# Expert rows weighted at eviction and added to the residual by an adding DMA, in a float32 hybrid-decoder layer

## What is computed

```python
x = x + mix                                    # residual after attention ("x2" in the kernel)
h = rms_norm(x, norm_ffn)                      # "h2"
g_probs = softmax(h @ w_group + b_group)       # 4 groups; top group g_idx with g_p = max
e_sel   = e_logits[tok, g_idx]                 # 8 experts of that group
top_v, top_i = lax.top_k(e_sel, 2)
top_w   = softmax(top_v) * g_p[:, None]        # the two weights of a token
# rows sorted by expert, every expert padded to blocks of 128 rows
yr = (silu(xb @ w_gate[e]) * (xb @ w_up[e])) @ w_down[e]
y  = zeros.at[row_tok].add(yr * row_w[:, None])
out = rms_norm(x + y, norm_final)
```

## Time and profile before

| | us |
|---|---|
| median of three runs | 2680.06 (2677.91 to 2688.39) |
| the profiled execution, its time | 2681.16 |
| its span from first to last instruction | 2679.6 |
| PE busy | 2340.3 (87%) |
| DVE busy | 1420.9 (53%) |
| ACT busy | 1188.9 (44%) |
| POOL busy | 663.5 (25%) |
| moved by DMA | 473.65 MB, 177 GB/s over the span |

### The profile page before, as it was taken

One profiled execution on the slowest core, in us unless ns is written; L12 is line 12 of the kernel. 1 busy time (PEld: TensorE's weight loads), 2 busy tenths in 40 slices (PEclk: granted clock), 3 DMA queues, 4 the chain that ended last, 5 costly groups with the idle time before them and its releaser, 6 DMA issues. The chain is left out here.

```text
span 2679.6 us, 36979 instructions
## 1 busy us (share of the span) xinstructions
PE 2340.3 (87%) x11480; PEld 1874.8 (70%) x11480; DVE 1420.9 (53%) x2814; ACT 1188.9 (44%) x1605; POOL 663.5 (25%) x464
## 2 busy tenths in 40 slices
PE   5999999994999999999959998399999999999920
PEld 3888889993666666666637887277888888787810
DVE  6212211004666666766634665476655565757656
ACT  5011111113666666667632222275555555556623
POOL 0000000003676666666600111110111111111133
PEclk7999999996999999999979998599999999999965
DMA  5333334215345453553145442579876776878668
GB/s 181 134 110 130 113 125 113 61 45 141 89 119 131 120 138 97 132 128 99 48 132 188 123 123 84 219 277 354 300 276 243 266 278 237 300 304 301 256 231 325
DMA packets 228011, 473.65 MB, mean 177 GB/s; under 512 B 20073, under 2 KB 72465, under 8 KB 225874
## 3 DMA queue, kind: packets, MB, share of 16 engines
q1 hardware_dynamic: 203026, 391.00, 43.7%
q0 software_dynamic: 17072, 53.79, 6.1%
q10 hardware_dynamic: 7824, 27.79, 2.8%
HBM read 355.30 MB, written 117.21 MB: 176 GB/s over the span
## 5 line engine op out<-in xcount | busy, mean ns | idle before, releaser
L1338 DVE TENSOR_TENSOR gu_lo<-gu_raw,gu_hi 128x2048 fp32r<-128x2048 f32 x128 | 293.2, 2291 | 130.9 <-issue 57.8
L584 DVE TENSOR_SCALAR_CACHE_REDUCE p_ring<-ps_s 128x256 f32<-128x256 f32 (+7 forms) x352 | 277.8, 793 | 156.3 <-PE ps_s L655 151.3
L521 POOL TENSOR_TENSOR p_ring<-p_ring 128x1152 f32<-128x1152 f32 (+15 forms) x128 | 322.1, 2516 | 10.7
L549 ACT ACTIVATE p_ring<-p_ring,shift 128x1152 f32<-128x1152 f32 (+15 forms) x256 | 305.9, 1197 | 27.2 <-DVE shift L600 27.2
L690 PE MATMUL ps_o<-aT,v_st 128*128 128x512 f32 (+3 forms) x640 | 291.1, 539 | 0.0
L1268 ACT ACTIVATE gu_hi<-gu_raw 128x2048 fp32r (+1 forms) x128 | 237.5, 1908 | 81.7 <-PE ps_g L1431 43.8
L538 ACT ACTIVATE aT<-ps_t 128x512 f32<-128x512 f32 (+1 forms) x320 | 168.3, 532 | 226.0 <-PE ps_t L675 225.9
L655 PE MATMUL ps_s<-k,q_st 128*128 128x512 f32 (+3 forms) x640 | 209.1, 454 | 45.8 <-DMA near<-near_rows 24.4
L1431 PE MATMUL ps_g<-gu_hi,xT_lo 128*128 128x512 f32 x720 | 231.8, 403 | 5.9 <-DVE xT_lo L1353 5.4
L1431 PE MATMUL ps_g<-gu_hi,xT_hi 128*128 128x512 f32 x720 | 227.8, 397 | 0.0
L1431 PE MATMUL ps_g<-gu_lo,xT_hi 128*128 128x512 f32 x720 | 227.7, 397 | 0.0
(11 more groups left out here) (224 smaller groups left out, 4211.2 us busy)
## 6 DMA issues: line engine op xcount, KB each, us to landing
gu_raw<-in_moe_w_gate SPq DMA_DIRECT2D x128, 512.0 KB, 11.7
gu_raw<-in_moe_w_up SPq DMA_DIRECT2D x128, 512.0 KB, 12.6
d_raw<-in_moe_w_down SPq DMA_DIRECT2D x64, 1024.0 KB, 5.0
qk<-stage SPq DMA_DIRECT2D x64, 512.0 KB, 2.8
q_st<-qk SPq DMA_DIRECT2D x128, 256.0 KB, 5.1
y_rows<-y_sb ACTq DMA_DIRECT2D x45, 512.0 KB, 6.9
y_rows<-nil SPq DMA_DIRECT2D x32, 512.0 KB, 6.1
w_raw<-in_diff_w_in POOLq DMA_DIRECT2D x12, 1024.0 KB, 6.8
```

Of the source, the lines that this page charges most:

```text
L521: pool.tensor_tensor(p0(r, 0, w), p0(r, 0, w), p1(r, 0, w), ALU.add).then_inc(mixed, 1)
L549: nc.scalar.activation(p, p, ACT.Exp, bias=shift[:, r % 8, m:m + 1], accum_out=sums[:, r % 8, m:m + 1]).then_inc(raised, 1)
L584: ins = nc.vector.tensor_scalar(p(r, k0, k0 + far), ps_s[:, c % 2, 0:far], SCALE, None, ALU.mult, ALU.max, accum_out=top[:, r % 4, m, col: ...
L1338: nc.vector.tensor_tensor(gu_lo[:, j * GC:(j + 1) * GC], raw(half, j), gu_hi[:, j * GC:(j + 1) * GC].bitcast(F32), ALU.subtract).then_inc( ...
```

## The change

Three groups of edits, made together.

**Weights early, in the lists.** An entry of `slots` is now a pair (token, weight). `choose` forms two differences on DVE (`x5`); ACT takes their exponential (`e5`) in the middle of its step, for tile n-5; `place` forms the sum, the reciprocal and the product and puts them beside the token (`tokw`). `kept`, `e_all`, `rank_all`, `start` and `dest` are no longer carried on, and three small copies in `choose` and one in `place` go. Empty entries are not zero but a dump row, 2048 plus a lane number, with weight 0; for that `h2` and `x2` get 128 more rows, which `attend` clears with two writes, and the 32 writes to `y` go, with `y` itself. The table has an eighth column.

**Adding in the expert stage.** `take_y` evicts with the row's weight as scale, and instead of the store POOL issues an indirect DMA that adds `y_sb` to the rows of `x2` that the list names. Because the list of block b+3 is loaded when block b+1 is added, lists wait in a line of five (`lists`), passed on by two POOL copies for each block (`pass_on`). `take_y` waits for these copies (`held`), and the copies wait for the add before (`y_out`). The transposes of the next block's rows move into the middle of `gate_up`.

**A shorter last stage.** `finish` loads all 16 tiles of `x2` at once, norms and stores them; no ring, no gathers, no weights.

```diff
@@ attend, SP
-            spare = scratch["y"].rearrange("(b p) d -> b p d", p=P)[EXPERTS:]
+            for dump in (scratch["h2"], scratch["x2"]):
+                sp.dma_start(dump[SEQ:SEQ + P].rearrange("p (k d) -> p k d", k=4),
+                             nil[:, :].unsqueeze(1).to_broadcast([P, 4, D // 4])).then_inc(nil_out, 16)
...
-                if n >= 0 and n % 9 == 5 and cleared < BLOCKS_MAX - EXPERTS:
-                    sp.dma_start(spare[cleared].rearrange("p (k d) -> p k d", k=4),
-                                 nil[:, :].unsqueeze(1).to_broadcast([P, 4, D // 4])).then_inc(nil_out, 16)
-                    cleared += 1
@@ mix_and_route, POOL
-            pool.memset(zeros[:, :], 0).then_inc(made, 1)
+            pool.memset(empty[:, :, :], 0).then_inc(made, 1)
...
+            pool.iota(lanes[:, :], pattern=[[1, SLOTS // P]], base=0, channel_multiplier=SLOTS // P).then_inc(made, 1)
...
+            pool.wait_ge(empty_set, 1)
@@ mix_and_route, ACT step
+                if has(at, 5):
+                    q = 1 - par
+                    act.wait_ge(chosen, (n - 5) * 13 + 13)
+                    nc.scalar.activation(e5[:, q, :], x5[:, q, :], ACT.Exp).then_inc(exped, 1)
+                if has(at, 0):
                     act.wait_ge(turned, n + (1 + TURNED0))
@@ mix_and_route, DVE choose and place
+                nc.vector.tensor_scalar(x5[:, q, 0:GROUPS_E], lg[:, 0:GROUPS_E], gm[:, 0:1], None, ALU.subtract)
...
+                nc.vector.tensor_tensor(x5[:, q, 4:5], ev[:, 1:2], ev[:, 0:1], ALU.subtract)
...
-                nc.vector.tensor_copy(kept[:, bass.ds(t, 1), 0:4].rearrange("p o n -> p (o n)"), lg[:, 0:4])
-                nc.vector.tensor_copy(kept[:, bass.ds(t, 1), 4:6].rearrange("p o n -> p (o n)"), ev[:, 0:2])
-                link(nc.vector.tensor_copy(e_all[:, bass.ds(t, 1), :].rearrange("p o n -> p (o n)"), eid[:, q, :]))
...
-                nc.vector.tensor_copy(rank_all[:, bass.ds(t, 1), :].rearrange("p o n -> p (o n)"), rank[:, q, :])
...
+                gate(dve, exped, t + 1, passed)
+                link(nc.vector.tensor_reduce(e_sum[:, :], e5[:, q, 0:GROUPS_E], AX.X, ALU.add))
+                link(nc.vector.scalar_tensor_tensor(out=den[:, :], in0=e5[:, q, 4:5], scalar=1.0, in1=e_sum[:, :],
+                                                    op0=ALU.add, op1=ALU.mult))
                 dve.wait_ge(freed, t + (FREED0 - 1))
-                link(nc.vector.tensor_copy(tok[:, q:q + 1], tok_f[:, 0:1]))
+                weight = tokw[:, q, :, 1].bitcast(F32)
+                link(nc.vector.reciprocal(weight[:, 0:1], den[:, :]))
+                link(nc.vector.tensor_tensor(weight[:, 1:2], weight[:, 0:1], e5[:, q, 4:5], ALU.mult))
+                nc.vector.tensor_copy(tokw[:, q, :, 0], tok_f[:, 0:1].to_broadcast([P, 2]))
@@ run_experts, POOL
+            def pass_on(count):
+                pool.tensor_copy(lists[:, 0:4, 0], lists[:, 1:5, 0]).then_inc(held, 1)
+                pool.tensor_copy(lists[:, 0:4, 1].bitcast(F32), lists[:, 1:5, 1].bitcast(F32)).then_inc(held, 1)
+                gate(pool, held, count * 2 + 1, passed)
+
+            def add_y(k):
+                gate(pool, y_taken, k + Y_TAKEN0, passed)
+                pool.indirect_dma_start(scratch["x2"], bass.IndirectOffsetOnAxis(ap=to_rows[:, 0:1], axis=0),
+                                        y_sb[:, :], None, compute_op=ALU.add).then_inc(y_out, 16)
...
+            for b in range(3):
+                load_x(b)
+                pass_on(b + 1)
+            load_x(3)
+            pass_on(4)
+            add_y(1)
+            with pool.Fori(1, most) as b:
+                load_x(b + 3)
+
+                gate(pool, y_out, b * 16, passed)
+                pass_on(b + 4)
+                add_y(b + 1)
@@ run_experts, ACT take_y (store_y goes)
-                act.wait_ge(y_out, k * 16 + (Y_OUT0 - 16))
-                nc.scalar.activation(y_sb[:, :], ps_y[:, :], ACT.Copy).then_inc(y_taken, 1)
+                act.wait_ge(held, k * 2 + 7)
+                nc.scalar.activation(y_sb[:, :], ps_y[:, :], ACT.Copy, scale=lists[:, 0, 1:2].bitcast(F32)).then_inc(y_taken, 1)
@@ run_experts, PE
                 for c in range(KC):
+                    if c == KC // 2 and ahead is not None:
+                        turn_x(ahead)
...
-                gate_up(b)
-                turn_x(b + 1)
+                gate_up(b, b + 1)
                 down(b)
@@ finish, SP (ACT and DVE: square, root, reciprocal, scale, for t in range(TILES))
+            for t in range(TILES):
+                sp.dma_start(acc[:, t, :], x2_rows[t]).then_inc(x_in[GROUPS[t]], 16)
...
+            for t in range(TILES):
                 gate(sp, done, t + 1, passed)
+                sp.dma_start(out_rows[t], acc[:, t, :]).then_inc(stored, 16)
```

More of the change, by code:

```diff
@@ L1189, in run_experts @@
         ps_y = ctx.enter_context(nc.psum_tensor("ps_y", [P, D], F32))
[L1190 removed]
+        ident = keep["ident"]
         s = lambda name: sem("d_" + name)
@@ L1256, in _ @@
                                         bass.IndirectOffsetOnAxis(ap=listed[:, 0:1], axis=0)).then_inc(x_in, 16)
+            def pass_on(count):
[6 more added lines that the diff above has]
+                                        y_sb[:, :], None, compute_op=ALU.add).then_inc(y_out, 16)
+            pool.memset(lists[:, :, :], 0).then_inc(held, 1)
+            pool.wait_ge(held, 1)
+            for b in range(3):
[9 more added lines that the diff above has]
+                add_y(b + 1)
+            for k in range(2):
+                gate(pool, y_out, most * 16 + k * 16, passed)
+                pass_on(most + (k + 4))
+                add_y(most + (k + 1))
+            gate(pool, y_out, most * 16 + 32, passed)
         @block.scalar
@@ L1311, in iteration @@
                 nc.scalar.activation(hT_hi[:, :], ps_h[:, :], ACT.Copy).then_inc(h_hi_set, 1)
-                if not first:
-                    store_y(b)
             gu_high(0, 0, None, range(GS))
@@ L1510, in _ @@
-            for i in range(RING):
-                load(i, i)
-            def store(t, i):
-                gate(sp, done, t + 1, passed)
-                sp.dma_start(out_rows[bass.ds(t, 1)].rearrange("o p d -> (o p) d"), acc[:, i, :]).then_inc(stored[i], 16)
-            with sp.Fori(0, TILES // RING - 1) as q:
-                for i in range(RING):
-                    store(q * RING + i, i)
-                    if i >= 1:
-                        load(q * RING + (RING + i - 1), i - 1)
-                load(q * RING + (2 * RING - 1), RING - 1)
```

197 lines of the change are left out of this document (55 added, 142 removed).

## The result

The changed kernel takes 2646.97 us (median; 2642.03 to 2649.18) where the kernel before takes 2680.2: ratio 0.9868, 95% interval 0.9854 to 0.9882. A second comparison of the same two kernels gave 2643.57 against 2682.53, ratio 0.9858 (0.9841 to 0.9874). The prediction was 2643, and its range 2624 to 2680 holds both. Whether its terms were right is another matter. Two of its errors nearly cancelled: 4.4 us too little for the last stage, 4.5 us too little for the end of the experts.

What follows compares the result with a forecast made beforehand. The prediction took PE to bound the routing steps and expert blocks, and transfers the last stage. Terms -52.9 + 3 + 0.5 + 4.8 + 4 + 3.7 = -36.9 us took the median 2680.06 to 2643, range 2624 to 2680.

Steps and rivals of the forecast that it cites:

- Last stage: Last stage, bound by transfers: without gathers 17.3 MB at 372 GB/s plus ends, 49.5 instead of 102.4 us, -52.9 us.
- End of the experts: End of expert stage: the last adding DMA takes 6 us from issue, delaying the next stage, +3 us (+1 to +9).
- Start of the experts and first early transposes: Expert start: POOL's extra table look and memset, +0.5 us; block 1: PE waits for x, then half clock, +4.8 us.
- Every block: Expert blocks: adding DMA, taken as 11 us, is free up to 13.5 us from issue; crowded blocks and list clashes +4 us.
- Routing: Routing steps: ACT's table loads and DVE's small operations, partly covered by DVE's 2.60 us idle, +3.7 us (+1 to +9).
- Attention: Attention stage: 32 writes of zeros go and two come, 0 us (-1 to +1).
- The slow adding DMA: Rival, expert blocks: adding DMA takes 15.2 to 17.4 us, x comes late in each block, 2714 to 2811 us; chance 0.11.
- The crowded one: Rival, expert blocks: adding DMA slow only where weights crowd the DMA engines, 20 to 40 us, 2659 to 2679; chance 0.10.
- The last stage at 300 GB/s: Rival, last stage: loads first and stores after reach only 300 GB/s each, 61 us, 2654 in all; chance 0.08.
- The drain: Rival, routing: a table load holds ACT twice its 1.28 us, +19.5 in place of +3.7 us, 2659; chance 0.03.
- The last stage paced by the chain of a tile: Rival, last stage: paced by each tile's chain, not bytes, staying near 90 us, 2681 in all; chance 0.02.
- The forecast's own case: Whole kernel: the summed terms hold, 2626 to 2662 us by their bounds; chance 0.66.

Runs made afterwards that it cites:

- stage without gathers: Kernel before with the last stage's 32 gathers and their waits removed, both weighted adds reading the row of final weights: 2660.1 us, stage 80.8 us.
- plain indirect DMA: Changed kernel with y written over the residual rows by the same indirect DMA without its addition: 2640.6 us, ratio 0.985.
- two at once: Changed kernel with a second, plain indirect DMA of the same y right behind each adding one, no wait between: 2661.3 us, ratio 0.9931.
- late transposes: Changed kernel with the transposes of the next block's x behind the gate and up products again, not in their middle: 2648.0 us, ratio 0.9876.
- Early root: Changed kernel with a small root of a constant on ACT behind each exponential, bringing the root's table back while ACT is idle: 2634.2 us, ratio 0.9818.
- early add: DVE's residual add moved before the low half of the transposed rows: kernel before 2656.6 us, changed kernel 2636.6 us, changed kernel with early root 2610.9 us.
- second execution: The changed kernel itself run and profiled once more, nothing changed: 2643.6 us, span of the profiled execution 2635.4 us.
- chain of two: Changed kernel with a second adding DMA of the same y into spare rows, issued once the first has landed: 2816.9 us, ratio 1.0513.

## Why the prediction was right, step by step

*Last stage*, -52.9 predicted, -57.3 found. The size came out and is the bulk of the gain. Bytes by rate was the right sum for the new stage: 17.3 MB at 388 GB/s are 44.6 us. The term was a little too small: 388 is the mean with the stage's ends in it, where 372 was taken and 3 us of ends added. Bytes by rate was not the whole reason. The prediction read a DMA share of 0.89 as "bound by its transfers" and would have promised the same for any edit that halves the bytes. The stage without gathers shows a second bound right behind, DVE and the ring at 81 us. Fewer bytes alone brought 21.6 us; the rest came with the weighted adds and the ring. DVE's busy 64 of 103 us in the earlier trace rows was the sign. In a stage of 50 us, 64 us of busy time can't fit; the prediction took the adds to be gone with the gathers, without saying that its result hung on that.

*End of the experts*, +3 predicted, +7.5 found: the mis-sized term. The adding DMA itself was guessed well, 6 us from issue, 6.3 measured. What failed is what stood around it: from the last y to the issue 1.9 us in place of 1.3, and from landing to the next stage 3.4 us where the plain store before had 0.4 (2574.23 + 2.6 to 2577.19). Of the plain indirect DMA the same is 2.5 us (issue at 2580.40, 3.5 to landing, next stage at 2586.40). So a good part of it comes with POOL's indirect DMA, adding or not. What those 2.5 to 3.4 us are stays open. By the Trainium skill (Collectives: The Full Stack, "The bandwidth ceiling"), the adding step of a ring collective reads two sources and ran at half the rate of a copy. Alone, the trace comes near that in the ratio of the two times (6.3 to 3.5, fixed parts included); among other traffic it does not (8.8 to 7.1).

*Start of the experts and first early transposes*, +0.5 and +4.8 predicted, together +6.0 and +2.1 found. Up to the first product it is +2.4 and +0.2: in the first execution the first list and its gather took longer, and the bounds of that term, -1 to +1.5, did not hold it. From there to the first y it is +3.5 and +1.9, and the mechanism is as told, one wait for xg and a stretch at half clock behind it. Both were in the first profiled execution (2.69 us, and 1.97 for the transposes instead of 1.03); in the second one the wait was 1.32 us and the transposes took 1.09.

*Every block*, +4 predicted, +3.4 and +3.9 found. That the size came out is luck. The term stood for crowded blocks whose adding DMA comes too late, and for clashes at the list; no y waits for POOL's copies, and without the addition the stage has the same 814.8 us. What changed are the periods of y: those of 18.75 and 17.43 us before are 19.24 and 16.98 us now, with and without the addition, those of the blocks at the start and of a few others are 0.1 to 0.2 us longer, and the last one 0.4 to 1.0. Which part of the change does that, no run says. The mechanism of the threshold can be checked all the same. Lists are 18.1 us apart in blocks without new weights, the adding DMA lands after 8.8 us in the median (11 was taken). The point from which it would cost was too high, though. It was put at 13.5 us; two at once, with the second in at 1.9 + 8.9 = 10.8 us from the first one's issue, already cost 13.4 us in all, though its added traffic may have a part in that. Two steps of the count failed. It let the list land at the moment when the adding DMA does, but it comes some 2 us later (2049.84 in the rows above, where the DMA before it is due at 2038.80 + 8.9). And it let `pass_on` wait for the adding DMA alone, where POOL's program has it behind the list and the gather's issue, as the late transposes showed. By that run the margin over the measured 8.8 us is at most 2 us, not 5.

*Routing*, +3.7 predicted. What was found depends on the execution. From the first load to the table's store, seven profiled executions with this routing code took 333.5, 333.5, 333.8, 334.0, 334.9, 334.9 and 340.6 us, two with the code of before 329.8 and 329.9. That is +4 in most, +10.7 in the one shown first; the prediction had +1 to +9. What it had right: 2.5 table loads in each step of the loop, 1.28 us each, the root 0.01 to 0.02 us behind, and PE waiting 0.63 us and more in turn. The Trainium skill (ScalarE: Activation LUTs, "What ACT_TABLE_LOAD costs") has 1.38 us of drain with each load; no trace here shows that. What it had wrong: it priced a wait of PE at its length. In every second step of the loop PE waited 0.88 or 1.78 us, not 1.0, and the row behind took up to 6.69 us instead of 5.5. Early root and early add show what the loads and the clock together were worth: 33 to 36 us against the changed kernel. On the other side, about 5 us came back at the end of the stage and were not foreseen: from the table's store to the next stage it is 4.2 and 3.8 us in place of 8.9. The last two pairs of scatters hold POOL up for less. Their rows have 8 bytes now, 4 before; whether that is the cause, no run shows. These 5 us are why the stage as a whole is no longer than before in the second execution.

*Attention*, 0 predicted, +2.5 and -0.2 found. The routing stage starts between 1363.4 and 1369.8 us in the fourteen profiled executions, whatever the kernel, so nothing of it is put down to the change.

*Rivals.* The slow adding DMA did not come, though the chain of two shows what it does when it does: 2817 us, a little over the 2714 to 2811. The crowded one: no. The last stage at 300 GB/s: no, 388. The drain: no. The last stage paced by the chain of a tile: no, 45.1 us. The forecast's own case was given as 2626 to 2662 by its bounds; added up, the bounds give 2622 to 2691, and how they were drawn together is not said.

## What to carry to other kernels

When an engine waits a little in each step, price the clock behind the wait and not only the wait: here 0.7 us of waiting cost 1.7 us in a step on average, and the cure was to move one add into idle time of the engine that was waited for. Put back a function table where the engine is idle, with a dummy operation, rather than let the next step fetch it on the chain. And before a stage's time is put down to bytes, sum the busy time of the next engine: the stage will not get below that.

## What the runs showed of the hardware

- TensorE's clock, in 105 rows of 16 products that open a projection, from seven traces (the kernel before, the changed kernel twice, and the four runs with the early root or the early add). A row took 3.9 us where the granted clock stayed at 2.4 GHz, and 5.3 to 6.8 us where it was at 1.2 GHz for a part; by the rows' lengths, the clock stayed up behind no wait, or one of up to 0.40 us, in all 32; behind 0.63 to 0.98 us in 14 of 44; behind 1.16 to 1.82 us in 4 of 18; behind 2.5 us and more in none of 11. So the length of the wait alone doesn't decide it. Routing stages with the same code took 333.5 to 340.6 us up to the table's store, with two rows of over 6.6 us in the slowest and one each in four others.
- An adding indirect DMA of 512 KB: 6.3 us from issue alone, 8.8 among other traffic, and 1.6 us of POOL for its issue; without the addition 3.5, 7.1 and 1.0. The DMA engines are busy for a share of 0.86 with the addition and 0.79 without it, at about the same bytes.
- Behind the landing of the last indirect DMA the next stage started 3.4 us (adding) and 2.5 us (plain) later, behind a plain store of ACT's queue 0.4, in one or a few traces each.
- Scattered rows of 4 bytes against 8: before, POOL waited 4.70 us for the one before last of the pairs, after 3.02 (3.26 in the second execution). This row of the kernel before and the one of the changed kernel show it; no run isolated it.

```profile
1693.37 0.96 POOL L905 DMA_INDIRECT slots<-tok,slot  x1 [4.70 <-DMA slots<-tok,slot]
```

```profile
1703.86 0.97 POOL L908 DMA_INDIRECT slots<-tokw,slot  x1 [3.02 <-DMA slots<-tokw,slot]
```
